# The places of a matmul kernel's SBUF tiles, modulo 512 bytes

## The chip, the cores and the metric

The kernel runs on one core of a Trainium2 chip. The metric is the device time of one execution in microseconds; lower is better.

## What is computed

Two model blocks run one after the other on x of 256 rows and 2048 columns, in fp32, each with two layers. A layer of the first block normalises x, projects it to 5,648 columns (2048 of them the gate z), runs sliding-window attention, spatial gating and gated linear attention on parts of them, and projects back:

```python
h = rms_norm(x, g_pre) * (1.0 + scale[:, None, :]) + shift[:, None, :]
proj = h @ w_in
y = jnp.concatenate([y_a, y_b, y_c], axis=-1) * jax.nn.silu(z)
out = y @ w_out
return x + gate[:, None, :] * rms_norm(out, g_post)
```

A layer of the second block is

```python
h = jnp.einsum('bsd,dc->bsc', x, w_in)
up_a = jnp.einsum('bsw,wd->bsd', out_a * jax.nn.silu(za), w_up_a)
up_b = jnp.einsum('bsw,wd->bsd', out_b * jax.nn.silu(zb), w_up_b)
y = jnp.einsum('bsd,de->bse', g_a * up_a + g_b * up_b, w_out)
return layer_norm(DEEPNORM_ALPHA * x + y, ln_g, ln_b)
```

with two attentions of 12 heads each for out_a and out_b, and a forget gate (12 columns of w_in) for the second. Nearly all of the arithmetic is in the products with the weight matrices.

## The kernel before

**Products in three passes.** A weight matrix is read in granules of 1024 columns by 128 partitions (two k-tiles of 512 output columns, 512 KB). For each granule, ScalarE makes whi, a rounded copy of raw in the float32r format (line 317 in the second block, 1413 in the first), and VectorE makes wlo = raw - whi (lines 434, 1638). The activations are kept the same way, transposed: xhi and xlo, ahi and alo in the second block, hhi and hlo in the first. TensorE adds three products, high by high, low by high and high by low, in PSUM. A matmul streams 512 columns of whi or wlo, against 128 columns of the activations' tile that are loaded first. A granule has 12 of them: three products, two k-tiles, two row blocks of 128:

```python
products = ((ahead, whi), (alow, whi), (ahead, wlo))
m = pe.matmul(acc[c % 2][:, tb, :], a[:, kk, tb * P:(tb + 1) * P],
              b[:, n % SLOTS, k * CW:(k + 1) * CW], ...)
```

That is `accumulate`, line 780; the first block has the same at line 2172. The first block has 240 granules, the second 672.

**Rings.** raw, whi and wlo each have SLOTS = 4 slots of 4096 bytes a partition; granule n uses slot n % 4. SyncE's queue loads raw when VectorE is through with a slot (s_lo), ScalarE writes a slot of whi when the matmuls of four granules ago are done (s_used), VectorE waits for s_hi, TensorE for s_hi and s_lo. The first block has two further slots, mraw, and reads the modulation matrix at its start in 32 tiles of 1 MB into b_y, mraw, scr and sgl (sgw and others are views of these).

**Order.** It is written out by hand: CHUNKS2 lists the column chunks of the second block, and `fills2` and `units2` say before which granule TensorE transposes tiles (lines 724 to 734, into psT) or does the attention's small products (lines 751, 761, psS). Line 768 is the forget gate: for each of 16 k-tiles it loads 12 columns of wfhi or wflo and streams 256 columns of xhi or xlo. Its tiles are 48 bytes apart. `fill_hi` (line 322) copies a transposed pair of tiles from psT to xhi, and line 440 makes xlo.

**Places.** SBUF tensors are laid one behind the other in the order of their making, rounded up to 32 bytes, and those of `program` (x, ident, raw, whi, wlo) stand first for both blocks. In the built program x begins at byte 16512 of each partition, which is 128 modulo 512. x has 16384 bytes, ident 512, the rings 16384 each, so that all of these, and hhi, hlo, b_y, mraw, scr in the first block and xhi, xlo, ahi, alo, y, gb and the tiles of the attention in the second, begin at 128 modulo 512. sgl begins at 160. wfhi begins at 384 and wflo at 128.

Of the kernel before, what the change touches and what calls it, by code (L numbers as in the profile page):

```python
# [17 lines left out]
F32R = mybir.dt.float32r  # L18
# [6 lines left out]
P = 128  # L25
SEQ = 256
TB = SEQ // P
D = 2048
KT = D // P
CW = 512  # L30
NCW = D // CW
GK = 2
SLOTS = 4
NEG = -1.0e30
DEPTH = 2

# [12 lines left out]
def at(layer, per_layer, count):  # L49

    return layer * per_layer + count
# [21 lines left out]
def granules2(c):  # L73
    return (FIRST2 + [GRAN2])[c + 1] - FIRST2[c]
# [55 lines left out]
LEAD = 2  # L130
CLOSING = (2, SLOTS)
PIECES = ((0, 0, 2 * CW), (0, 2 * CW, 2 * CW), (1, 0, 2 * CW), (1, 2 * CW, CW), (1, 3 * CW, CW))


def second_block(nc, ctx, x, rings, ps, dram, s_w, ident):


    raw, whi, wlo = rings
# [4 lines left out]
    def sb(name, shape, dt=F32):  # L143
        return ctx.enter_context(nc.sbuf_tensor(name, shape, dt))
# [1 line left out]
    def sem(name):  # L146
        return ctx.enter_context(nc.semaphore(name))

    xhi = sb("xhi", [P, KT, SEQ], F32R)
    xlo = sb("xlo", [P, KT, SEQ], F32R)  # L150
    ahi = sb("ahi", [P, KT_UP, SEQ], F32R)
    alo = sb("alo", [P, KT_UP, SEQ], F32R)
# [84 lines left out]
    def multiplied(l, c):  # L237

        return s_used, at(l, GRAN2, SLOTS + FIRST2[c] + granules2(c))

# [31 lines left out]
    @block.sync  # L272
    def _(sp):
        with sp.Fori(1, DEPTH * GRAN2 // SLOTS) as i:
            for b in range(SLOTS):
                src = dram["w"][sp.snap(i * SLOTS + b)]
                sp.wait_ge(s_lo, i * SLOTS + b - SLOTS + 1)
                sp.dma_start(raw[:, b, :], src).then_inc(s_w[b], 16)
        for i, (tb, start, width) in enumerate(PIECES):
            sp.wait_ge(s_fin, i + 1)  # L280
            sp.dma_start(dram["out"][tb * P:(tb + 1) * P, start:start + width],
                         x[:, tb, start:start + width]).then_inc(s_out, 16)
        sp.wait_ge(s_out, 16 * len(PIECES))
# [570 lines left out]
def rope_tables():  # L854

    half = HD // 2
    inv = (np.float32(10000.0) ** (-np.arange(half, dtype=np.float32) / half)).astype(np.float32)
    ang = (np.arange(SEQ, dtype=np.float32)[:, None] * inv[None, :]).astype(np.float32).astype(np.float64)
    t = np.stack([np.cos(ang), np.sin(ang), -np.sin(ang)])
    t = np.stack([t * SCALE2, t]).reshape(2, 3, TB, P, half).transpose(3, 0, 1, 2, 4)  # L860
    return np.ascontiguousarray(t.astype(np.float32))


def band(weight):

    t, s = np.arange(P)[:, None], np.arange(SEQ)[None, :]
    return np.concatenate([weight(t - s[:, :P]), weight(t + P - s)], axis=1).astype(np.float32)


def constants():  # L870
# [5 lines left out]

        "mask_a": band(lambda d: np.where(count(d) > 0, np.log(np.maximum(count(d), 1)), NEG)),
        "mask_b": band(lambda d: np.where(d >= 0, 0.0, NEG)),
        "tables": rope_tables(),
# [1305 lines left out]
def first_constants():  # L2185
# [7 lines left out]
    for m in LEVELS[1:]:  # L2193
# [8 lines left out]
        "lmask": np.stack(masks, axis=1).astype(np.uint8),  # L2202
        "mask_w": band(lambda d: np.where((d >= 0) & (d < WINDOW), 0.0, NEG)),
    }
# [63 lines left out]
def program(nc, dram):  # L2268
    with ExitStack() as ctx:
        def sb(name, shape, dt=F32):  # L2270
            return ctx.enter_context(nc.sbuf_tensor(name, shape, dt))

        x = sb("x", [P, TB, D])
        ident = sb("ident", [P, P])
        rings = (sb("raw", [P, SLOTS, GK * CW]), sb("whi", [P, SLOTS, GK * CW], F32R),
                 sb("wlo", [P, SLOTS, GK * CW], F32R))
        acc = [ctx.enter_context(nc.psum_tensor(f"acc{i}", [P, TB, CW], F32)) for i in range(2)]
        psT = ctx.enter_context(nc.psum_tensor("psT", [P, TB, CW], F32))
        psS = ctx.enter_context(nc.psum_tensor("psS", [P, TB, CW], F32))
        s_w = [ctx.enter_context(nc.semaphore(f"c_w{i}")) for i in range(SLOTS)]  # L2280
        with ExitStack() as first:
            first_block(nc, first, x, rings, (acc, psT, psS), dram, ident, s_w)
        with ExitStack() as second:
            second_block(nc, second, x, rings, (acc, psT, psS), dram, s_w, ident)
# [22 lines left out]
```

## Time and profile before

| | us |
|---|---|
| median of 3 runs | 2887.79 |
| lowest to highest | 2884.63 to 2889.06 |
| the profiled execution | 2884.92 |
| its span, first to last instruction | 2883.2 |
| TensorE busy | 2797.1 (97%) |
| VectorE busy | 1792.1 (62%) |
| ScalarE busy | 1374.5 (48%) |
| mean granted TensorE clock | 0.988 |

Busy times of TensorE overlap for matmuls that are in the array together, so the mean duration of one (some 390 ns) is not its pace; the pace is the distance of starts, or the time of a run of matmuls in the chain by its count. A granted clock of 1.00 is 2.4 GHz, 0.50 is 1.2 GHz. The first block ends at about 887 us.

### The profile page before, as it was taken

The page shows a single profiled execution, that of the slowest core. Times are in us where ns is not written, and L with a number is a line of the kernel's source. Part 1 is how long each engine was busy: PE and PEld are TensorE (multiplying, and loading weights), DVE is VectorE, ACT ScalarE, POOL GpSimd, SP SyncE. Part 2 cuts the span into 40 slices and gives each one's busy share as a digit, 9 for nine tenths or more (in the row PEclk, how much of TensorE's full clock was granted, in tenths as well). Part 3 has the DMA queues.
Part 4 walks back from the last instruction along what each step waited for, and adds up shares of the span by engine and source line. Part 5 has one row for each costly group of instructions (what it writes and reads, how often), then busy time and mean ns, then how long its engine had stood idle before and what let it go on. Part 6 is the DMA issues. An engine that isn't in the chain of part 4 may idle for free.

```text
span 2883.2 us, 35735 instructions
## 1 busy us (share of the span) xinstructions
PE 2797.1 (97%) x13346; PEld 2316.9 (80%) x13346; DVE 1792.1 (62%) x2195; ACT 1374.5 (48%) x1785; POOL 36.2 (1%) x69
## 2 busy tenths in 40 slices
PE   6799998999998999999999999999999999999998
PEld 5678786888887888888888888878888888888886
DVE  6979898768755555555445556575565545445565
ACT  4355545555544444443545544344445445545443
POOL 0000000000000000000000000000000000000000
PEclk9999999999999999999999999999999999999999
DMA  9987697865654555466555565645555665555564
GB/s 383 354 300 249 206 361 299 311 224 184 207 194 156 170 179 178 158 226 193 177 181 168 175 197 193 222 164 170 177 172 171 224 194 170 178 178 173 196 215 146
DMA packets 159991, 603.73 MB, mean 209 GB/s; under 512 B 18376, under 2 KB 18576, under 8 KB 154464
## 3 DMA queue, kind: packets, MB, share of 16 engines
q1 hardware_dynamic: 155376, 583.08, 59.3%
q0 software_dynamic: 4464, 18.55, 2.1%
q8 instruction: 106, 1.74, 0.2%
q14 instruction: 45, 0.37, 0.0%
HBM read 599.41 MB, written 2.14 MB: 209 GB/s over the span
## 4 chain that ended last, share of the span: by engine, by line
PE 68%; DVE 1%; ACT 0%; DMA 0%; issue 0%; SPq 0%; ACTq 0%; DVEq 0%
PE acc L780 63%; PE psT L728 2%; PE psS L761 1%; PE psS L751 1%; PE psT L734 1%; PE psS L768 0%; DMA raw<-in_w 0%; DVE wlo L434 0%; ACT whi L317 0%; DVE x L487 0%; DVE x L486 0%; PE psT L724 0%; DVE x L468 0%; DVE x L470 0%; DVE stats L453 0%
## 5 line engine op out<-in xcount | busy, mean ns | idle before, releaser
L434 DVE TENSOR_TENSOR wlo<-raw,whi 128x1024 fp32r<-128x1024 f32 x672 | 822.5, 1225 | 866.1 <-ACT whi L317 864.6
L317 ACT ACTIVATE whi<-raw 128x1024 fp32r<-128x1024 f32 x672 | 711.4, 1059 | 995.8 <-PE acc L780 980.0
L780 PE MATMUL acc<-whi,xhi 128*128 128x512 f32 x2304 | 638.0, 398 | 2.5 <-DVE xlo L440 1.5
L780 PE MATMUL acc<-whi,xlo 128*128 128x512 f32 x2304 | 619.5, 390 | 0.0
L780 PE MATMUL acc<-wlo,xhi 128*128 128x512 f32 x2304 | 619.3, 390 | 0.0
L780 PEld LDWEIGHTS acc<-whi,xlo 128*128 128x128 f32 x2304 | 433.1, 188 | 92.4
L780 PEld LDWEIGHTS acc<-wlo,xhi 128*128 128x128 f32 x2304 | 433.1, 188 | 91.6
L780 PEld LDWEIGHTS acc<-whi,xhi 128*128 128x128 f32 x2304 | 423.0, 189 | 83.5 <-DVE xlo L440 3.5
L1413 ACT ACTIVATE whi<-raw 128x1024 fp32r<-128x1024 f32 x177 | 186.7, 1058 | 266.6 <-PE acc L2172 158.8
L2172 PE MATMUL acc<-whi,hhi 128*128 128x512 f32 x864 | 247.9, 409 | 32.1 <-DVE hlo L1649 32.1
L1638 DVE TENSOR_TENSOR wlo<-raw,whi 128x1024 fp32r<-128x1024 f32 x177 | 215.1, 1222 | 90.2 <-ACT whi L1413 89.6
L2172 PE MATMUL acc<-whi,hlo 128*128 128x512 f32 x864 | 238.1, 398 | 0.0
L2172 PE MATMUL acc<-wlo,hhi 128*128 128x512 f32 x864 | 235.1, 394 | 0.0
L2172 PEld LDWEIGHTS acc<-whi,hhi 128*128 128x128 f32 x864 | 157.7, 192 | 70.1 <-DVE hlo L1649 35.7
L2172 PEld LDWEIGHTS acc<-whi,hlo 128*128 128x128 f32 x864 | 166.4, 193 | 36.8
L2172 PEld LDWEIGHTS acc<-wlo,hhi 128*128 128x128 f32 x864 | 165.2, 191 | 35.7
L1413 ACT ACTIVATE whi<-mraw 128x1024 fp32r<-128x1024 f32 x63 | 66.7, 1058 | 82.1 <-PE acc L2172 62.1
L780 PE MATMUL acc<-whi,ahi 128*128 128x512 f32 x384 | 103.2, 391 | 0.0
L780 PE MATMUL acc<-wlo,ahi 128*128 128x512 f32 x384 | 102.7, 389 | 0.0
L780 PE MATMUL acc<-whi,alo 128*128 128x512 f32 x384 | 102.7, 389 | 0.0
L1638 DVE TENSOR_TENSOR wlo<-mraw,whi 128x1024 fp32r<-128x1024 f32 x63 | 77.1, 1224 | 38.1 <-ACT whi L1413 38.0
L1663 DVE SCALAR_TENSOR_TENSOR raw<-raw,crow 128x1024 f32<-128x1024 f32 x79 | 96.8, 1225 | 1.1 <-DMA raw<-in_w_late 0.3
(321 smaller groups left out, 2135.8 us busy)
## 6 DMA issues: line engine op xcount, KB each, us to landing
raw<-in_w SPq DMA_DIRECT2D x849, 512.0 KB, 3.4
raw<-in_w_late SPq DMA_DIRECT2D x79, 512.0 KB, 5.1
mraw<-in_w SPq DMA_DIRECT2D x63, 512.0 KB, 4.8
mraw<-in_w_late SPq DMA_DIRECT2D x49, 512.0 KB, 4.7
b_y<-in_w_early SPq DMA_DIRECT2D x12, 1024.0 KB, 8.6
mraw<-in_w_early SPq DMA_DIRECT2D x7, 1024.0 KB, 8.7
scr<-in_w_early SPq DMA_DIRECT2D x7, 1024.0 KB, 9.0
sgl<-in_w_early SPq DMA_DIRECT2D x6, 1024.0 KB, 9.5
```

The source lines that it names most:

```text
L317: act.activation(whi[:, n % SLOTS, :], raw[:, n % SLOTS, :], ACT.Copy).then_inc(s_hi, 1)
L434: dve.tensor_tensor(wlo[:, n % SLOTS, :], raw[:, n % SLOTS, :], whi[:, n % SLOTS, :].bitcast(F32), ALU.subtract).then_inc(s_lo, 1)
L728: t = pe.transpose(bank[:, k * SEQ + tb * P:k * SEQ + (tb + 1) * P], src[:, tb, col + k * P:col + (k + 1) * P], ident[:])
L734: t = pe.transpose(bank[:, k * P:(k + 1) * P], prob[:, name[2], k * P:(k + 1) * P], ident[:])
L751: m = pe.matmul(out, qT[:, h, tb * P:(tb + 1) * P], kT[:, h, 0:w], start=True, stop=True)
L761: m = pe.matmul(bank[:, h * HD:(h + 1) * HD], probT[:, u, col * P:(col + 1) * P], v[:, s, h * HD:(h + 1) * HD], start=(s == 0), stop=(s == ...
L780: m = pe.matmul(acc[c % 2][:, tb, :], a[:, kk, tb * P:(tb + 1) * P], b[:, n % SLOTS, k * CW:(k + 1) * CW], start=(kk == 0 and q == 0), sto ...
L1413: act.activation(whi[:, n % SLOTS, :], slot(("w", n)), ACT.Copy).then_inc(s_hi, 1)
L1638: dve.tensor_tensor(wlo[:, n % SLOTS, :], slot(("w", n)), whi[:, n % SLOTS, :].bitcast(F32), ALU.subtract).then_inc(s_lo, 1)
L1663: dve.scalar_tensor_tensor(out=slot(("m", i)), in0=slot(("m", i)), scalar=1.0, in1=crow[:, part * MOD_W:(part + 1) * MOD_W], op0=ALU.mult, ...
L2172: m = pe.matmul(bank_a(gc)[:, tb, :], a[:, kt, tile], b[:, n % SLOTS, k * CW:(k + 1) * CW], start=(g == 0 and k == 0 and q == 0), stop=(g ...
```

## The change

```diff
--- before.py
+++ after.py
@@ -31,6 +31,7 @@
 NCW = D // CW
 GK = 2
 SLOTS = 4
+LINE = 128
 NEG = -1.0e30
 DEPTH = 2
 
@@ -146,7 +147,7 @@
     def sem(name):
         return ctx.enter_context(nc.semaphore(name))
 
-    xhi = sb("xhi", [P, KT, SEQ], F32R)
+    xhi = sb("xhi", [P, KT, SEQ + LINE // 8], F32R)[:, :, 0:SEQ]
     xlo = sb("xlo", [P, KT, SEQ], F32R)
     ahi = sb("ahi", [P, KT_UP, SEQ], F32R)
     alo = sb("alo", [P, KT_UP, SEQ], F32R)
@@ -2270,10 +2271,11 @@
         def sb(name, shape, dt=F32):
             return ctx.enter_context(nc.sbuf_tensor(name, shape, dt))
 
+        sb("border", [P, LINE // 4 * 3])
         x = sb("x", [P, TB, D])
         ident = sb("ident", [P, P])
-        rings = (sb("raw", [P, SLOTS, GK * CW]), sb("whi", [P, SLOTS, GK * CW], F32R),
-                 sb("wlo", [P, SLOTS, GK * CW], F32R))
+        rings = (sb("raw", [P, SLOTS, GK * CW]), sb("whi", [P, SLOTS, GK * CW + LINE // 4], F32R)[:, :, 0:GK * CW],
+                 sb("wlo", [P, SLOTS, GK * CW + LINE // 8], F32R)[:, :, 0:GK * CW])
         acc = [ctx.enter_context(nc.psum_tensor(f"acc{i}", [P, TB, CW], F32)) for i in range(2)]
         psT = ctx.enter_context(nc.psum_tensor("psT", [P, TB, CW], F32))
         psS = ctx.enter_context(nc.psum_tensor("psS", [P, TB, CW], F32))
```

- A tensor `border` of 384 bytes, which nothing reads or writes, stands in front of x: x, ident and raw begin at 0 modulo 512 in place of 128.
- A slot of whi is 4224 bytes, of which the first 4096 are used: the slots begin at 0, 128, 256 and 384.
- A slot of wlo is 4160 bytes: 0, 64, 128 and 192.
- All that follows in either block is 1152 bytes further on, at 256 modulo 512 in place of 128 (sgl at 288).
- A k-tile of xhi is 1088 bytes, of which 1024 are used: the 16 tiles run through 256, 320, 384, 448, 0, 64 and so on, and what follows xhi in the second block is another 1024 bytes further on, still at 256.
- xlo, ahi, alo, hhi and hlo keep tiles that are multiples of 512 apart.

In the built program every engine has the same instructions in the same order with the same waits. Of the 10944 matmuls that stream 512 columns of whi or wlo, all had both operands at the same place modulo 512 before; now 1536 have. The streamed operand begins at 0 or 128 in 2736 matmuls each, at 256 or 384 in 1824 each, and at 64 or 192 in 912 each. One form changes: a copy to two tiles of xhi no longer writes one run of 512 elements. On ScalarE, at the start of the second block (xhi<-psT is the copy of transposed x, whi<-raw that of a granule), before:

```order
L322 ACTIVATE xhi<-psT 128x4x128
L317 ACTIVATE whi<-raw 128x1024
L322 ACTIVATE xhi<-psT 128x512
L317 ACTIVATE whi<-raw 128x1024
L322 ACTIVATE xhi<-psT 128x512
L317 ACTIVATE whi<-raw 128x1024
```

and now:

```order
L323 ACTIVATE xhi<-psT 128x4x128
L318 ACTIVATE whi<-raw 128x1024
L323 ACTIVATE xhi<-psT 128x2x256
L318 ACTIVATE whi<-raw 128x1024
L323 ACTIVATE xhi<-psT 128x2x256
L318 ACTIVATE whi<-raw 128x1024
```

The copies of two tiles, 28 in the program, write 2 runs of 256; the first fills of x wrote 4 runs of 128 already.

## Rows read from the trace of the kernel before

**Rows 1.** The page, parts 1 and 2, whole span.
```profile
PE 2797.1 (97%) x13346; PEld 2316.9 (80%) x13346; DVE 1792.1 (62%) x2195; ACT 1374.5 (48%) x1785; POOL 36.2 (1%) x69
...
PEclk9999999999999999999999999999999999999999
```

**Rows 2.** The waits, whole span: engine, line, waited for: us in total, times, longest.
```profile
ACT whi L317 <- PE acc L780: 980.0, 613, 6.7
DVE wlo L434 <- ACT whi L317: 864.6, 599, 5.3
...
PE acc L2172 <- DVE hlo L1649: 32.1, 9, 5.0
```

**Rows 3.** The page, part 5: three of the groups of 512-column matmuls.
```profile
L780 PE MATMUL acc<-whi,xhi 128*128 128x512 f32 x2304 | 638.0, 398 | 2.5 <-DVE xlo L440 1.5
...
L2172 PE MATMUL acc<-whi,hhi 128*128 128x512 f32 x864 | 247.9, 409 | 32.1 <-DVE hlo L1649 32.1
...
L780 PE MATMUL acc<-whi,ahi 128*128 128x512 f32 x384 | 103.2, 391 | 0.0
```

**Rows 4.** The chain, 1200 to 1400 us: start us, us, what.
```profile
1211.01 5.46 PE psS L768 x48
1216.47 163.23 PE acc L780 x720
```

**Rows 5.** By stretch: length, PE, PEld, DVE, ACT, POOL busy, clock, DMA share, GB/s.
```profile
28.90:33.40 4.50, 0.07 (x1) 0.07 (x1) 2.05 (x3) 4.47 (x7) 0.00 (x0) 0.99 1.01 421
1216.47:1379.70 163.23, 163.23 (x723) 135.09 (x722) 84.41 (x74) 73.09 (x70) 2.71 (x5) 1.00 0.63 203
84.00:88.00 4.00, 4.00 (x10) 3.13 (x11) 4.00 (x4) 0.00 (x0) 0.28 (x1) 0.50 1.02 390
```

**Rows 6.** The timeline of TensorE, 84 to 88 us.
```profile
85.71 1.91 PE L2172 MATMUL acc<-whi,hlo 128*128 128x512 f32 x4
87.42 0.89 PE L2172 MATMUL acc<-wlo,hhi 128*128 128x512 f32 x2
```

**Rows 7.** The groups of weight loads, whole span.
```profile
L780 PEld LDWEIGHTS acc<-wlo,xhi 128*128 128x128 f32 x2304 | 433.1, 188 | 91.6
...
L2058 PEld LDWEIGHTS psT<-av,scr 128*128 128x128 f32 x192 | 22.7, 192 | 0.6
...
L2065 PEld LDWEIGHTS psT<-b_stage,sgl 128*128 128x128 f32 x64 | 7.5, 192 | 0.4 <-DVE rt L1945 0.4
...
L768 PEld LDWEIGHTS psS<-xhi,wfhi 128*12 128x12 f32 x32 | 2.9, 91 | 0.8
```

**Rows 8.** The chain, 900 to 920 us.
```profile
904.84 0.44 PE psT L728 x4
905.28 2.77 PE acc L780 x12
```

**Rows 9.** Tiles whi, wlo in 28:34, 1220:1380, 96:104, 1220:1380; ns minimum/median/maximum.
```profile
L1413 ACT ACTIVATE whi<-raw x4: 1040/1044/1047, 28.9 to 33.4; 128x1024 fp32r<-128x1024 f32 x4
...
L317 ACT ACTIVATE whi<-raw x60: 1042/1060/1063, 1219.3 to 1379.8; 128x1024 fp32r<-128x1024 f32 x60
...
L1638 DVE TENSOR_TENSOR wlo<-raw,whi x4: 1217/1218/1218, 96.4 to 102.7; 128x1024 fp32r<-128x1024 f32 x4
...
L434 DVE TENSOR_TENSOR wlo<-raw,whi x59: 1218/1225/1226, 1220.4 to 1378.2; 128x1024 fp32r<-128x1024 f32 x59
```

**Rows 10.** By stretch, as in rows 5, two of the first block.
```profile
0.00:150.00 150.00, 106.44 (x413) 82.88 (x414) 119.32 (x147) 60.64 (x76) 10.39 (x23) 0.92 0.93 361
200.00:560.00 360.00, 343.52 (x1761) 284.74 (x1760) 315.47 (x512) 191.36 (x299) 6.92 (x12) 0.97 0.81 288
```

**Rows 11.** Tile xhi on ScalarE, whole span; ns as in rows 9.
```profile
L322 ACT ACTIVATE xhi<-psT x32: 588/597/600, 892.2 to 2791.8; 128x512 fp32r<-128x512 f32 x32
```

**Rows 12.** The page, part 6: 1 MB loads, us to landing.
```profile
b_y<-in_w_early SPq DMA_DIRECT2D x12, 1024.0 KB, 8.6
...
sgl<-in_w_early SPq DMA_DIRECT2D x6, 1024.0 KB, 9.5
```

## The prediction

> **What bounds the kernel now.** I read the profile's page first: TensorE is busy for 2797.1 us of 2883.2 us (97%), and the granted clock is nine tenths or more in every slice [rows 1]. So the time is the number of matmuls times their pace, and only what changes that pace, or opens gaps on TensorE, counts. The waits confirm it: ScalarE waits 980.0 us for TensorE's matmuls of line 780 and VectorE 864.6 us for ScalarE, while TensorE's own longest wait in total is 32.1 us, all of it in the first block [rows 2]. The second block, from about 892 us, is a TensorE stream with almost nothing between.
>
> The costliest groups are the 512-column matmuls on whi and wlo [rows 3]: 3 x 2304 against xhi and xlo, 3 x 384 against ahi and alo, 3 x 864 against hhi and hlo in the acc banks, and 288 more of these in psS and psT. The loops give the same: 912 granules of 12, **10944** matmuls. Their pace is best read in the chain, where 720 of them follow each other in 163.23 us [rows 4]: **226.7 ns each**. At 2.4 GHz, with the granted clock 1.00 there [rows 5], 512 columns are 213.3 ns. So 13.4 ns, 5.9% of each, is something other than a column per cycle. At the other level, clock 0.50 [rows 5], four such matmuls start 1.71 us apart [rows 6]: 427.5 ns each, and 512 columns at 1.2 GHz are 426.7 ns. The extra is there at the full clock alone, so it looks like the supply of operands rather than a fixed cost, and that makes the placement of the operands worth an argument.
>
> **The change part by part.** No instruction is added, removed or moved, and no wait. Only addresses change, and the shape of 28 copies.
>
> 1. **TensorE's two reads.** Before, whi, wlo, xhi, xlo, ahi, alo, hhi and hlo all start at 128 modulo 512 bytes, and every slot, tile and half is a multiple of 512: in all 10944 matmuls the streamed operand and the loaded one begin at the same place modulo 512. After, 1536 still do (xhi, the ring's slots and hhi happen to agree), 9408 differ by 64 to 448. If the 13.4 ns are a collision of these two reads, up to 9408 x 13.4 ns = 126 us are to be had. Do the rows say so? The nearest rows are the forget gate's matmuls of line 768, 48 in each layer: they stream 256 columns of xhi or xlo and load 12 columns of wfhi or wflo, whose tiles step by 48 bytes and so already run through the places modulo 512. The 48 take 5.46 us [rows 4], 113.8 ns each, 7.1 ns above the 106.7 ns of 256 columns. The extra is halved with the streamed columns, although a tenth of the columns is loaded (12 against 128; the load lasts 91 ns against 188 ns [rows 7]) and although the places differ. So it goes with the streamed columns, 0.026 and 0.028 ns per column, and not with the load or with the distance of the two places. The streamed operand reads alone, and its own alignment to 128 bytes is kept in whi. I take **0 us**. Ends: 126 us less (whole collision), and, for the other sign, the worst pace that is seen with a full clock in a stretch: 12 matmuls right behind four transposes take 2.77 us [rows 8], 230.8 ns each, 4.1 ns above the settled pace; on 9408 that is 39 us more.
>
> 2. **wlo's odd slots** start at 64 modulo 128. 2 KB then touch 17 stretches of 128 bytes in place of 16. If the 13.4 ns were paid by the stretch, 1824 matmuls would pay 0.84 ns more: 1.5 us. I take 0.
>
> 3. **Loads at another place.** sgl starts at 160 modulo 512 (32 modulo 128), scr at 128; loads of 128 columns from either last 192 ns [rows 7]. No cost.
>
> 4. **The copies of ScalarE and VectorE.** whi<-raw takes 1060 ns in the median under a full stream of matmuls and 1044 ns where TensorE is all but idle [rows 5, 9]; wlo<-raw,whi takes 1225 ns under the stream and 1218 ns in a stretch of the first block with a wait of TensorE in it [rows 9]. So the engines do touch each other in SBUF, by 16 and 7 ns. The ends are these amounts on every copy, lost or regained: 912 granules are 15 us on ScalarE and 6 us on VectorE. In the second block both wait for TensorE by hundreds of us [rows 2], so it costs nothing there; that cover would be gone only if copies grew by more than their slack, and a granule's 12 matmuls are 2.72 us against 1.23 us. In the first block VectorE is busy for 315 of 360 us from 200 to 560 us [rows 10] and 240 of the granules lie there: 7 ns x 240 = **1.7 us**, either way. I take 0.
>  The Trainium skill, page SBUF — State Buffer, section "SBUF: two separate sides", says that TensorE and ScalarE never wait on anyone there. The trace does not quite agree: 16 ns per copy. By the page this term is exactly zero and placement can matter to no engine, which is the same result here but for a stronger reason.
>
> 5. **xhi's tiles have gaps**, so the 28 copies xhi<-psT of two tiles write 2 x 256 in place of 512. The fills of x's first four tiles already write 4 x 128 and last 588 to 600 ns like all 32 [rows 11]: 0 us. Even 10 ns each would be 0.3 us.
>
> 6. **DMA.** raw moves from 128 to 0 modulo 512, mraw, b_y and scr from 128 to 256, sgl from 160 to 288: their places modulo 128 stay. No packet changes. The 1 MB transfers to b_y land in 8.6 us and those to sgl, at 160, in 9.5 us [rows 12], the only pair with different places, with the queue's state mixed in. If a place cost that 10%, the 32 early tiles (32 MB, some 90 us at the 361 GB/s of the first 150 us) would move by 9 us, down or up, in the stretch where DMA is 93% busy [rows 10]. The unchanged place modulo 128 lets me take 0.
>
> The sum is 0 us on the profiled execution's 2884.9 us; the median of the runs is 2.9 us above it, and I forecast **2888 us**, that median. A measurement here tells about 0.2% (5.8 us) from no change; this is 0.5 ns per matmul, so even a small dependence of the pace on placement would be seen.
>
> **The rivals.**
>
> *The placement decides the pace (faster).* The two reads of TensorE meet in the same part of SBUF because they begin at the same place, and 9408 matmuls lose their 13.4 ns: 2762 us against the median. For it: the extra vanishes at half the clock, where reads have twice the time. Against it: line 768, with nearly no load. A smaller form: only one product in three gains, the 3648 matmuls that stream wlo, of which all but 288 begin elsewhere than their load: 49 us, 2839 us. I give 0.12 to the whole and 0.10 to the smaller, which is also what is left to gains I have not named.
>  The Trainium skill, page TensorE: Matmul & The Clock Gate, section "Back-to-back issue gap", gives N / 2.4 + 2.5 ns when warm, which is 215.8 ns for 512 columns; the trace has 226.7. By that page 10.9 ns are not inherent, and if this placement freed them the time would be some 103 us less.
>
> *Equal places are the good case (slower).* TensorE settles into 226.7 ns with equal places; just behind transposes, whose reads are at other rates, it does not yet [rows 8]. If the settled pace needs equal places, each of the 9408 stays at about 230.8 ns: 39 us, 2927 us, or half of it, 2907 us, if every second one does. It decides from 0.6 ns per changed matmul (5.8 us / 9408). For it: the pace is that exact in every long stretch, and the placement was equal in all of them. Against it: line 768 again, at its exact pace with mixed places. 0.19, with 0.05 more for a slower first block (steps 4 and 6, 11 us together).
>
> *The change does not do what it says.* The addresses in the built program are as described, so I give it nothing of its own.
>
> **How the numbers follow.** No change has 0.54 (2882 to 2893 us, its own range with the spread of the runs), faster 0.22, slower 0.24. The range from 2839 to 2927 us leaves out the whole collision (0.12) and little above.
>
> **What would show it.** In the changed profile: the 720 matmuls of the long stretch still in 163.2 us; the groups of line 780 (781 there) with means of 390 to 398 ns; loads at 188 ns; the copies at 1060 and 1225 ns; xhi<-psT at 597 ns. I am wrong if the long stretch takes 154 us (the reads collided) or 166 us (equal places were good), or if matmuls on one slot of the ring keep another pace than those on the next.

## The result, and the profile after

| | before | after |
|---|---|---|
| median | 2887.83 us (4 runs) | **2928.40 us** (4 runs) |
| lowest to highest | 2884.63 to 2889.06 | 2925.92 to 2929.86 |
| profiled execution, its span | 2884.92, 2883.2 | 2925.92, 2924.2 |
| TensorE busy | 2797.1 | 2838.4 |

The ratio is **1.0139**, with a 95% interval from 1.0126 to 1.0152. The change costs 40.6 us where no change was forecast, and the median lies just above the forecast range, which ended at 2927 us.

The page of the changed kernel, parts 1 and 2:

```profile
PE 2838.4 (97%) x13346; PEld 2321.1 (79%) x13346; DVE 1792.8 (61%) x2195; ACT 1375.1 (47%) x1785; POOL 36.6 (1%) x69
...
PEclk9899999999999999999999999999999999999999
```

TensorE is busy for 41.3 us more than in [rows 1], and the span is 41.0 us longer: the whole loss is TensorE's. VectorE and ScalarE are as busy as before to within 0.7 us. The granted clock is the same, but for one slice with an 8 in place of a 9 in the first block.

Part 5, the nine groups of 512-column matmuls in the acc banks (busy us, mean ns of one):

```profile
L781 PE MATMUL acc<-whi,xhi 128*128 128x512 f32 x2304 | 644.1, 401 | 2.5 <-DVE xlo L441 1.5
L781 PE MATMUL acc<-whi,xlo 128*128 128x512 f32 x2304 | 630.6, 395 | 0.0
L781 PE MATMUL acc<-wlo,xhi 128*128 128x512 f32 x2304 | 627.8, 393 | 0.0
...
L2173 PE MATMUL acc<-whi,hhi 128*128 128x512 f32 x864 | 250.3, 412 | 31.5 <-DVE hlo L1650 31.5
...
L2173 PE MATMUL acc<-whi,hlo 128*128 128x512 f32 x864 | 241.5, 402 | 0.0
L2173 PE MATMUL acc<-wlo,hhi 128*128 128x512 f32 x864 | 239.2, 399 | 0.0
...
L781 PE MATMUL acc<-whi,ahi 128*128 128x512 f32 x384 | 105.2, 395 | 0.0
L781 PE MATMUL acc<-wlo,ahi 128*128 128x512 f32 x384 | 104.2, 393 | 0.0
L781 PE MATMUL acc<-whi,alo 128*128 128x512 f32 x384 | 104.0, 393 | 0.0
```

Three of them answer to [rows 3]: 644.1 us against 638.0, 250.3 against 247.9, 105.2 against 103.2. All nine grow, by 2.4 to 11.1 us for those on the large tiles, and together by 40.4 us. The six others stood, in the order shown, at 619.5, 619.3, 238.1, 235.1, 102.7 and 102.7 us in the page of before.

The chain of waits, around the long stretch:

```profile
1224.99 5.60 PE psS L769 x48
1230.59 166.31 PE acc L781 x720
1396.89 0.87 PE psT L729 x8
1397.77 22.21 PE acc L781 x96
...
1429.19 0.89 PE psS L752 x8
1430.09 2.78 PE acc L781 x12
```

The 720 matmuls that took 163.23 us [rows 4] now take 166.31 us: 231.0 ns each in place of 226.7, 4.3 ns more. The run of 12 right behind small products shown here takes 2.78 us, beside the 2.77 us of [rows 8]. Over 82 such runs of 12 in the second block, taken from the trace by their starts, the cost is 2.0 ns a matmul: they were unsettled before too, and lose about half of what the long stretch loses. The forget gate's 48 matmuls take 5.60 us, 0.14 us more.

What the prediction left at zero beside TensorE's pace is indeed unchanged. The tiles whi, wlo (1230 to 1396 us) and xhi (whole span), ns minimum/median/maximum as in [rows 9] and [rows 11]:

```profile
L318 ACT ACTIVATE whi<-raw x59: 1039/1061/1064, 1233.5 to 1394.2; 128x1024 fp32r<-128x1024 f32 x59
```

```profile
L435 DVE TENSOR_TENSOR wlo<-raw,whi x59: 1219/1226/1227, 1234.6 to 1395.3; 128x1024 fp32r<-128x1024 f32 x59
```

```profile
L323 ACT ACTIVATE xhi<-psT x32: 587/597/601, 902.2 to 2831.2; 128x512 fp32r<-128x512 f32 x32
```

### The profile page after: what moved, and what is told of

Same layout as the page of the kernel before. It is cut to its first block, busy times and chain, and to the rows that moved or that the text cites. A ratio compares the mean times of both kernels' runs of the same rounds, so it can differ in the third digit from the quotient of the medians.

```text
span 2924.2 us, 35735 instructions
## 1 busy us (share of the span) xinstructions
PE 2838.4 (97%) x13346; PEld 2321.1 (79%) x13346; DVE 1792.8 (61%) x2195; ACT 1375.1 (47%) x1785; POOL 36.6 (1%) x69
## 4 chain that ended last, share of the span: by engine, by line
PE 68%; DVE 1%; ACT 0%; issue 0%; DVEq 0%; ACTq 0%
PE acc L781 64%; PE psT L729 2%; PE psS L762 1%; PE psS L752 1%; PE psT L735 1%; PE psS L769 0%; DVE x L471 0%; DVE x L469 0%; DVE x L488 0%; DVE x L487 0%; PE psT L725 0%; DVE stats L454 0%; DVE x L447 0%; DVE xlo L441 0%; ACT whi L318 0%
## 5 line engine op out<-in xcount | busy, mean ns | idle before, releaser
L435 DVE TENSOR_TENSOR wlo<-raw,whi 128x1024 fp32r<-128x1024 f32 x672 | 822.7, 1225 | 896.5 <-ACT whi L318 894.5
L781 PE MATMUL acc<-whi,xhi 128*128 128x512 f32 x2304 | 644.1, 401 | 2.5 <-DVE xlo L441 1.5
L781 PE MATMUL acc<-whi,xlo 128*128 128x512 f32 x2304 | 630.6, 395 | 0.0
L781 PE MATMUL acc<-wlo,xhi 128*128 128x512 f32 x2304 | 627.8, 393 | 0.0
L2173 PE MATMUL acc<-whi,hhi 128*128 128x512 f32 x864 | 250.3, 412 | 31.5 <-DVE hlo L1650 31.5
L781 PE MATMUL acc<-whi,ahi 128*128 128x512 f32 x384 | 105.2, 395 | 0.0
L1639 DVE TENSOR_TENSOR wlo<-mraw,whi 128x1024 fp32r<-128x1024 f32 x63 | 77.1, 1224 | 40.4 <-ACT whi L1414 40.1
```

Of the source, the lines that this page charges most:

```text
L435: dve.tensor_tensor(wlo[:, n % SLOTS, :], raw[:, n % SLOTS, :], whi[:, n % SLOTS, :].bitcast(F32), ALU.subtract).then_inc(s_lo, 1)
L1639: dve.tensor_tensor(wlo[:, n % SLOTS, :], slot(("w", n)), whi[:, n % SLOTS, :].bitcast(F32), ALU.subtract).then_inc(s_lo, 1)
L2173: m = pe.matmul(bank_a(gc)[:, tb, :], a[:, kt, tile], b[:, n % SLOTS, k * CW:(k + 1) * CW], start=(g == 0 and k == 0 and q == 0), stop=(g ...
```

## The experiments

Four theories were at hand. **A**: what counts is the distance of the loaded operand's place from the streamed one's, modulo 256 bytes; at 0 the pace is 226.7 ns. It came from the changed kernel's trace, taken granule by granule: where whi's slot and the loaded tiles were 0 or 256 apart, the matmuls settled at 226 to 228 ns; where they were 128 apart, at 238 and 229 ns in turn. (That is the prediction's last sign of being wrong: another pace on one slot of the ring than on the next.) **B**: the places must be equal modulo 512. **C**: the absolute place counts, and 128 was a good one. **D**: what costs is the jump of a place from one matmul to the next.

Where this section gives a pace of a group, it is the mean distance of starts between 512-column matmuls with at least eight others ahead of them, out of the trace.

### One distance everywhere

All have the border of 384 bytes, rings without pads, and no jumps. e2 and e3 add a pad in front of the loaded tiles, 32 or 64 floats:

```diff
+        sb("border", [P, 96])
         x = sb("x", [P, TB, D])
@@ first_block, and the same in front of xhi (not in e1) @@
+    sb("border3", [P, 32])
     hhi = sb("hhi", [P, KT, SEQ], F32R)
```

> The border of 384 bytes alone: every operand at 0 modulo 512 in place of 128, all still at equal places. Theory A (the distance of the loaded operand's place from the streamed one's, modulo 256, sets the pace; it is 0 here): 226.7 ns per matmul, 2885 to 2891 us. Theory B (the two places must be equal modulo 512): the same. Theory C (the absolute place matters, and 128 modulo 512 was a good one): slower, up to the 40 us of the change. Theory D (what costs is the jump of a place from one matmul to the next, not the distance): the same as before.

> Every streamed operand at 0, every loaded one at 128 modulo 512, no pads inside rings or tiles, so that nothing jumps. Theory A, from the changed kernel's granules whose places were 128 apart (238 and 228 ns in turn, 233.3 on average): 233.3 ns per matmul in the long stretch, 10944 x 6.6 ns = 72 us more, 2955 to 2963 us. Theory B: slower as well, no number. Theory C: as e1. Theory D: 226.7 ns, 2885 to 2891 us.

> As e2_apart128, with 256 in place of 128. Theory A (modulo 256 only): 226.7 ns, 2885 to 2891 us. Theory B (modulo 512): slower, by 20 us or more. Theory D: 2885 to 2891 us.

| | streamed, loaded | median us | ratio to before, 95% | long stretch |
|---|---|---|---|---|
| e1_border | 0, 0 | 2888.30 | 1.0000 (0.9991 to 1.0010) | 163.23 us |
| e2_apart128 | 0, 128 | 2941.00 | 1.0184 (1.0167 to 1.0201) | 167.31 us |
| e3_apart256 | 0, 256 | 2887.28 | 0.9995 (0.9985 to 1.0005) | 163.23 us |

The long stretch in the chain of e2_apart128, then of e3_apart256, with the forget gate ahead of it:

```profile
1229.58 5.46 PE psS L769 x48
1235.04 167.31 PE acc L781 x720
```

```profile
1214.57 5.46 PE psS L769 x48
1220.03 163.23 PE acc L781 x720
```

C and D fall: at another absolute place nothing changes, and with a constant distance of 128 and no jump at all the kernel loses 53 us, more than the change. B falls with e3. A stands, though its sum for e2 was too high by 14 us or more. The pace was a little lower than the 233.3 ns assumed (232.8 ns on the tiles xhi and xlo), and the runs of 12 right behind small products pay 2.9 ns a matmul in e2, about half of the 6.1 ns that the settled ones pay.

### The change in parts, and jumps without a distance

```diff
@@ p_whi @@
+        whi = sb("whi", [P, SLOTS, GK * CW + 32], F32R)[:, :, 0:GK * CW]
@@ p_wlo @@
+        wlo = sb("wlo", [P, SLOTS, GK * CW + 16], F32R)[:, :, 0:GK * CW]
@@ p_xhi @@
+    xhi = sb("xhi", [P, KT, SEQ + 16], F32R)[:, :, 0:SEQ]
@@ f_whi256 @@
+        whi = sb("whi", [P, SLOTS, GK * CW + 64], F32R)[:, :, 0:GK * CW]
```

> Of the change, whi's slots of 4224 bytes alone (with the border). whi begins at 0, 128, 256, 384, everything else at 0. Theory A (a matmul costs more where the loaded place is not 0 modulo 256 from the streamed one): half of the slots are 128 off, in two products of three: 3648 matmuls x 6.1 ns (the 232.8 ns of e2_apart128) = 22 us more, 2905 to 2915 us. If the places cost by their jumps (theory D), whatever the distance: 2 of 12 matmuls per granule, under 10 us.

> Of the change, wlo's slots of 4160 bytes alone (with the border). wlo begins at 0, 64, 128, 192, the loaded tiles at 256. Theory A: one product of three, three slots of four off by 64, 128 or 192: 2736 matmuls x 3 to 7 ns = 8 to 19 us more, 2897 to 2907 us.

> Of the change, xhi's tiles of 1088 bytes alone (with the border). Theory A: the 4608 matmuls against xhi, three of four off by 64, 128 or 192: 3456 x 3 to 7 ns = 10 to 24 us more, 2898 to 2912 us. The first block and the matmuls on xlo, ahi and alo keep 226.7 ns.

> As p_whi, with 256 bytes in place of 128: whi's slots begin at 0 and 256 in turn, so that places jump between slots and between whi and wlo, but every distance is 0 modulo 256. Theory A: 226.7 ns, no change, 2884 to 2891 us. Theory D (jumps cost): as much as p_whi, 2905 us or more.

| | median us | ratio to before, 95% | long stretch |
|---|---|---|---|
| p_whi | 2911.78 | 1.0079 (1.0062 to 1.0095) | 165.03 us |
| p_wlo | 2909.55 | 1.0074 (1.0057 to 1.0091) | 165.20 us |
| p_xhi | 2917.22 | 1.0095 (1.0078 to 1.0112) | 165.63 us |
| f_whi256 | 2888.05 | 0.9997 (0.9988 to 1.0007) | 163.23 us |

Each pad alone costs, 22.9, 20.7 and 28.3 us against 2888.88 us of before in the same job. Together that is 72 us, the change 40.6 us: the parts do not add, since each pad also moves the distance that another makes. Counted from the layouts, 3648, 2736 and 3456 matmuls have a distance that is no multiple of 256, 9840 in all, but in the change only 6384. That explains a part; per such matmul the three cost 6.3, 7.6 and 8.2 ns and the change 6.4 ns, and why these differ was not tested. f_whi256 has jumps of 256 bytes between slots and keeps its 226.7 ns, the clearest word against D.

p_wlo and p_xhi came out above their bounds, and the paces show why. In p_xhi the products with xlo have distance 0 and still keep 231.4 ns; in p_wlo the products of whi by xhi, distance 256, keep 230.0 ns and those of whi by xlo behind them 227.4. p_whi shows it by slots of whi (second block, position by position): where whi is 128 apart, the four products with wlo behind it have distance 0 and still keep 232, 232, 231 and 227 ns, and the next granule, all at distance 0, has 227 ns from its first matmul on. A matmul does not pay for its own distance alone: what a disturbed product leaves lasts through the next several matmuls. The groups of p_xhi show where it reaches (part 5):

```profile
L780 PE MATMUL acc<-whi,xlo 128*128 128x512 f32 x2304 | 628.8, 394 | 0.0
...
L2172 PE MATMUL acc<-whi,hlo 128*128 128x512 f32 x864 | 237.8, 398 | 0.0
```

### Other distances

e4_survey has slots 32 bytes apart in their places:

```diff
+        whi = sb("whi", [P, SLOTS, GK * CW + 8], F32R)[:, :, 0:GK * CW]
+        sb("border2", [P, 96])
+        wlo = sb("wlo", [P, SLOTS, GK * CW + 8], F32R)[:, :, 0:GK * CW]
```

> A survey in one program: the slots of whi and of wlo begin at 0, 32, 64 and 96, both alike; hhi and hlo at 0, xhi and xlo at 128, ahi and alo at 256. Within a granule nothing jumps, and the distances are 0 to -96 (first block), 128 to 32 (xhi, xlo) and 256 to 160 (ahi, alo) in steps of 32. Theory A: granules at distance 0 and 256 at 226.7 ns per matmul, at 128 at 233.3 ns, and between them at 227 to 234 ns, alike for d and 256 - d; in time some 30 to 60 us over before. Theory D: all granules at 226.7 ns but for their first matmuls.

It took 2940.85 us, with 230 to 234 ns in every kind of granule. In those at distance 0 or 256 only the last three of the 12 matmuls were back at 227 ns. So a survey by slots is spoilt by what the slot before leaves, and theory A's "226.7 ns for granules at distance 0" missed for that reason. The four others keep one distance per tile, by a shift inside the tensor; g1 for instance (the border of 384 bytes is in all four, so that the streamed operand stays at 0, and only the loaded tiles move):

```diff
+    xhi = sb("xhi", [P, KT * SEQ + 128], F32R)[:, 16:16 + KT * SEQ].rearrange("p (k t) -> p k t", k=KT)
```

> Three constant distances in one program, nothing jumps: hhi and hlo 16 bytes, xhi and xlo 64, ahi and alo 96 beyond the streamed operand's place, which is 0. Theory A as it stands gives no pace between 0 and 128: e4_survey has 233 to 234 ns for odd multiples of 32 and 229.7 ns for -64, polluted by the slots before. Expected: 16 at 228 to 234 ns, 64 at 229 to 233 ns, 96 at 233 to 234 ns; 2920 to 2945 us. Rival: some distance is better than 0, below 226.7 ns, since 213.3 ns would be a column per cycle.

> As g1_16_64_96, with hhi and hlo 240 bytes (-16 modulo 256), xhi and xlo 192 (-64), ahi and alo 32 beyond the streamed operand's place. Expected: 240 at 228 to 234 ns, 192 at 229 to 231 ns, 32 at 233 to 234 ns; 2910 to 2935 us. Same rival: a pace below 226.7 ns at one of them.

> Three more constant distances: hhi and hlo 8 bytes beyond the streamed place, xhi and xlo 224, ahi and alo 160. If the pace is a smooth function of the distance through the nine known (0: 226.7, 16: 230.9, 32: 233.3, 64: 233.3, 96: 234.3, 128: 232.7, 192: 229.0, 240: 227.9, 256: 226.7): 8 at 227 to 230 ns, 224 at 227.5 to 229 ns, 160 at 230 to 232 ns, about 2905 to 2915 us. Rival: one of them is below 226.7 ns, and a placement faster than both kernels exists.

> The last three distances: hhi and hlo 248 bytes beyond the streamed place (8 short of 256), xhi and xlo 208, ahi and alo 144. The curve is not smooth: 8 costs as much as 16 (230.7 and 230.9 ns), 224 has 233.3 ns between 192 with 229.0 and 240 with 227.9. If only multiples of 256 are free: all three at 227.5 to 234 ns. Rival: a distance just short of 256 is below 226.7 ns, because 240 is the best of the others.

One execution each: 2942.77, 2910.00, 2938.26 and 2937.73 us, beside 2886.4 to 2889.8 us of before. Pace by distance in bytes modulo 256, with e2 and e3:

| distance | 0 | 8 | 16 | 32 | 64 | 96 | 128 | 144 | 160 | 192 | 208 | 224 | 240 | 248 |
|---|---|---|---|---|---|---|---|---|---|---|---|---|---|---|
| ns | 226.7 | 230.7 | 230.9 | 233.3 | 233.3 | 234.2 | 232.8 | 232.0 | 233.3 | 228.9 | 232.3 | 233.3 | 227.9 | 233.3 |

**None of the 13 is below 0's**, and the curve is not smooth: g3's expectation from neighbouring distances missed on all three, 8, 224 and 160. g4's own, three paces between 227.5 and 234 ns, held, and so did g1's and g2's but for 0.1 to 0.3 ns at 64, 96, 192 and 240. A version faster than both kernels was not found in placement. One rival is left: for 128 bytes, distance and place are told apart (both operands at 128 keep 226.7 ns in the kernel before), but for the 12 others only the loaded tiles were moved in g1 to g4, so the cost there may belong to the loaded tile's own place as well as to the distance. In the chain, 96 matmuls on xhi and xlo take 22.40 us at 64 (233.3 ns each) and 21.98 us at 192 (229.0 ns), in g1 and g2:

```profile
942.53 22.40 PE acc L780 x96
```

```profile
938.21 21.98 PE acc L780 x96
```

The means hide two states at some distances. TensorE's timeline of g1_16_64_96 in the first block, at distance 16 (start us, us, then the form; each row is four matmuls):

```profile
641.80 1.10 PE L2172 MATMUL acc<-wlo,hhi 128*128 128x512 f32 x4
642.74 1.09 PE L2172 MATMUL acc<-whi,hhi 128*128 128x512 f32 x4
643.67 1.10 PE L2172 MATMUL acc<-whi,hlo 128*128 128x512 f32 x4
644.60 1.08 PE L2172 MATMUL acc<-wlo,hhi 128*128 128x512 f32 x4
...
646.51 1.16 PE L2111 MATMUL psS<-zt 64*128 64x128 f32 x16
647.60 1.19 PE L2172 MATMUL acc<-whi,hhi 128*128 128x512 f32 x4
648.62 1.07 PE L2172 MATMUL acc<-whi,hlo 128*128 128x512 f32 x4
649.53 1.07 PE L2172 MATMUL acc<-wlo,hhi 128*128 128x512 f32 x4
650.44 1.07 PE L2172 MATMUL acc<-whi,hhi 128*128 128x512 f32 x4
651.34 1.07 PE L2172 MATMUL acc<-whi,hlo 128*128 128x512 f32 x4
652.25 1.07 PE L2172 MATMUL acc<-wlo,hhi 128*128 128x512 f32 x4
```

From 641.80 to 644.60 us the rows start 0.93 us apart, 233.3 ns a matmul. From 649.53 to 652.25 us, on the same tiles at the same distance, they start 0.907 us apart, 226.7 ns. Which of the two a stretch gets is settled at its entry, behind small products or a wait, and then holds: of the 146 granules of the first block that follow another one without small products between, 52 keep 226.5 to 227 ns and 86 keep 233 to 233.5; the other eight are slower. What decides at the entry is open: two stretches of 324 matmuls behind the same kind of transposes, from 403 and from 819 us, keep 233.5 and 226.7 ns.

Distance 16 is not alone. At 144 (g4), 18 of 90 such granules on ahi and alo keep 226.6 ns and 72 keep 233 to 233.5; at 240 (g2), 38 of 146 keep 226.7 ns and 99 keep 228.3. So the means at 16, 144 and 240 depend on how this kernel's stretches happen to be entered. Two rows of g4 at 144, start to start, are 0.91 us apart, and two others 0.93 us:

```profile
1768.15 1.07 PE L780 MATMUL acc<-whi,ahi 128*128 128x512 f32 x4
1769.06 1.07 PE L780 MATMUL acc<-whi,alo 128*128 128x512 f32 x4
```

```profile
1803.19 1.09 PE L780 MATMUL acc<-whi,ahi 128*128 128x512 f32 x4
1804.12 1.10 PE L780 MATMUL acc<-whi,alo 128*128 128x512 f32 x4
```

### Less to load beside the stream

```diff
+                    cols = P // 4 if q == 1 else P
-                    m = pe.matmul(acc[c % 2][:, tb, :], a[:, kk, tb * P:(tb + 1) * P],
+                    m = pe.matmul(acc[c % 2][0:cols, tb, :], a[:, kk, tb * P:tb * P + cols],
```

> Equal places (all at 0), and in the second block the product with xlo and alo loads 32 columns in place of 128 (rows 32 to 127 of each row block lose that product). Theory L (the 13.4 ns over a column per cycle are a collision of the stream with the load of the next tile, in proportion to what is loaded): the matmuls beside which a narrow load runs keep 213.3 + 13.4/4 = 216.7 ns, so the groups on xlo and alo fall to about 219 ns on average; 4 matmuls of 12 in 672 granules gain 10 ns, 27 us less, about 2861 us. Theory S (the prediction's step 1: the extra belongs to the streamed columns alone, whatever is loaded): 226.7 ns as before, 2885 to 2892 us.

> As h1_narrow with every loaded operand 128 bytes from the streamed one's place. Theory L: the matmuls beside a narrow load keep 213.3 + 19.5/4 = 218 ns (19.5 ns being the extra of e2_apart128), the others 232.8 ns; about 2901 us against the 2941 us of e2_apart128. Theory S with a separate price for the distance: 226.7 to 228 ns beside a narrow load.

> As h1_narrow with 64 columns loaded for the products with xlo and alo in place of 32 (rows 64 to 127 lose that product); all places 0. h1_narrow was slower, not faster: 232.2 ns on the narrow groups. Theory E (stream and load stay in step where the load begins at the stream's place modulo 256 and also covers a multiple of 256 bytes, so that it ends in step; 128 columns are 512 bytes, 64 are 256, 32 only 128): 226.7 ns throughout, 2885 to 2892 us. Theory W (any load that is narrower than 128 columns, or any change of width, disturbs): 229 to 233 ns on these groups, 2905 to 2920 us. Theory L, fallen with h1_narrow, would have 220 ns.

One execution each: 2917.71, 2937.59 and 2906.77 us. Loading less did not free anything. Groups of loads of h1_narrow (a narrow load lasts 108 ns, a full one 188 ns), and the long stretches of h1 and h3:

```profile
L781 PEld LDWEIGHTS acc<-wlo,xhi 128*128 128x128 f32 x2304 | 434.0, 188 | 149.1 <-DVE wlo L434 0.3 <-issue 0.3
...
L781 PEld LDWEIGHTS acc<-whi,xlo 128*32 128x32 f32 x2304 | 249.2, 108 | 235.2 <-issue 0.5
```

```profile
1225.03 166.18 PE acc L781 x720
```

```profile
1223.16 165.19 PE acc L781 x720
```

With 32 columns the products with xlo keep 232.2 ns, with 64 columns 230.0 ns, and in both the products with wlo behind them 231 ns. Theory L falls: the 13.4 ns are no loss in proportion to what is loaded. Theory S falls as well: with the same streamed columns at equal places the pace changed. The edit does not show that it is the load that did it, for a matmul on 32 or 64 loaded columns also writes only as many rows of acc. Theory E falls with h3, whose loads of 64 columns cover 256 bytes (its W range, 229 to 233 ns, held). W, that any narrower product or change of width disturbs, is all that the three leave, and it names no mechanism. At distance 128, h2's narrow loads gave 3.4 us back, within what one execution tells.

## Why the prediction was wrong

- **The bound** was right: TensorE's pace times the number of matmuls. All of the 41.0 us is in TensorE's busy time.
- **Step 1 failed.** It took 0 us for the two reads, since line 768 "goes with the streamed columns, and not with the load or with the distance of the two places". Two things were wrong in it. The rows of line 768 stream 256 columns beside a load of 12, and such a matmul is no stand-in for 512 beside 128: the forget gate kept 5.46 us even in e2_apart128, while the long stretch behind it went from 163.23 to 167.31 us. Nor was it free of placement: with xhi's tiles of 1088 bytes, which it streams, it took 5.60 us in the change and 5.61 us in p_xhi. And a ratio of two extras, 7.1 to 13.4 ns, was read as a mechanism when it had been seen at two sizes. The row said nothing of another distance beside a full load, and e2 shows what that costs: 232.8 ns in place of 226.7 ns on xhi and xlo.
- The same step's upper end was the answer: "230.8 ns, 4.1 ns above the settled pace; on 9408 that is 39 us more". Measured were 231.0 ns in the long stretch and 40.6 us. The rival that used it, "Equal places are the good case", gave 2927 us and had a chance of 0.19. Its place and its sign were right. Its condition was too narrow: not equal places, but places apart by a multiple of 256 bytes (e3, f_whi256). That the price came out so well is in large part luck: it is 9408 x 4.1 ns by the rival and 6384 x 6.4 ns by the distances modulo 256. The paces run from 227.9 to 234.2 ns by distance, the runs of 12 behind small products pay about half, and some matmuls that keep distance 0 pay with their neighbours. The 4.1 ns themselves were the excess of unsettled matmuls at distance 0, not a price of any distance.
- The other rival, a collision at equal places, had the sign wrong: equal places are the best of 14. Its argument, that the extra is absent at half the clock, still holds as an observation. Its smaller form was also added up wrongly: without the 288 matmuls that it leaves out, 3360 x 13.4 ns are 45 us, not 49.
 The Trainium skill, page TensorE: Matmul & The Clock Gate, section "Back-to-back issue gap", gives N / 2.4 + 2.5 ns for the isolated gap at the full clock, 215.8 ns here. No run came near it for these float32r matmuls; some 226.7 ns was the lowest pace that any stretch settled at.
- **Steps 3 to 6** were right at 0 or could not be told from it: the copies still take 1061 and 1226 ns, xhi<-psT 597 ns, VectorE's and ScalarE's busy times moved by 0.7 and 0.6 us, and in the first 150 us DMA moved 360 GB/s after 361. Step 2, a price of wlo's slots at 64 modulo 128 on its own, stays open: p_wlo cost 20.7 us, but its slots change the distance too.
 Step 4 weighed what the Trainium skill, page SBUF — State Buffer, section "SBUF: two separate sides", says of TensorE and ScalarE never waiting. The prediction drew from it that placement can matter to no engine. For the copies the trace bears that out (1061 and 1226 ns after, 1060 and 1225 ns before); for TensorE it does not: 231.0 ns after, 226.7 ns before.
- **What stood against the forecast in plain sight:** every one of the 10944 matmuls had the same distance, 0. The trace of before held no case of what the change would make; the slower matmuls of [rows 8] too had distance 0, and showed only that a slower pace exists. With only that to go by, "no change" deserved less than 0.54.

What stays open is the mechanism: why a stream of 512 float32r columns settles at 226.7 ns at one distance and at up to 234.2 ns at others, and why a distance of 0 modulo 256 with full loads found the faster pace in every long stretch of before, e1, e3 and f_whi256.

## What to carry to other kernels

Where TensorE streams 512 float32r columns against loads of 128 back to back, keep the streamed and the loaded operand's places apart by a multiple of 256 bytes, slots and k-tiles included; any pad in a ring or a tile should be a multiple of 256, since a distance of 128 throughout costs 1.8% of the whole kernel (e2_apart128), and a pad of 64 or 128 in a single ring or tile 0.7 to 1.0% (p_wlo, p_whi, p_xhi). An even layout that nobody chose may be the reason for an even pace, and a trace in which all cases are alike says nothing of the others. Measure a constant distance per tile, not one that changes by slot: what one granule disturbs, the next one pays for.

## What the runs showed of the hardware

- The pace of 512-column float32r matmuls at the full clock depends on the distance of the two operands' places modulo 256 bytes: 226.7 ns at 0, 227.9 to 234.2 ns on average at 13 others. With both operands at 0 or both at 128 the pace is the same; at the 12 others only the loaded tile was moved.
- At one distance there can be two settled paces: 226.7 and some 233.3 ns at 16 and at 144 bytes, 226.7 and 228.3 ns at 240. Each stretch of g1, behind its entry, keeps one of them while nothing interrupts it.
- Narrower products, in loaded columns and in rows written, made the stream slower: 230.0 ns with 64 and 232.2 ns with 32, at equal places.
